# SBUF start addresses: where the moving operands of the matmuls begin within 128 bytes

## The reference, cut to what matters

```
first, for each of 2 layers:
  z = rms_norm(h) @ w_in                       # 1024 -> 2624
  y = [latent attention(z), retention(z)]      # w_q_b, w_kv_b inside
  h = h + y @ w_out
  h = h + (silu(hf @ gate) * (hf @ up)) @ w_down     # hf = rms_norm(h), 2816 wide
second, layer 0:  FFN, pooling mixer (pool_w), FFN   # each FFN 1024 -> 2*2816 -> 1024
second, layer 1:  FFN, differential attention (qkv, w_o), FFN
out = rms_norm(x, final_g)
```

## The kernel before

| tile | before | after |
|---|---|---|
| raw, w_hi, w_lo, R | 0 | 0 |
| xn_hi, xn_lo, sqb, tn, ssum | 0 | 64 |
| tab (constants) | 32 | 96 |
| mid_hi, mid_lo | 0 | 64 |
| dq, dk, oh, ol (second attention) | 64 | 64 |
| lat, zq, zk, zv (first attention), zp | 64 | 0 |
| krp, qf, v_ret | 0 | 64 |
| cn_hi, cn_lo (first row) | 0 | 0 |

## Time and profile before

### The profile page before, as it was taken

One profiled execution on the slowest core, in us unless ns is written; L12 is line 12 of the kernel. 1 busy time (PEld: TensorE's weight loads), 2 busy tenths in 40 slices (PEclk: granted clock), 3 DMA queues, 4 the chain that ended last, 5 costly groups with the idle time before them and its releaser, 6 DMA issues.

```text
span 2301.2 us, 37388 instructions
## 1 busy us (share of the span) xinstructions
PE 2258.3 (98%) x14172; PEld 2033.1 (88%) x14172; DVE 1462.8 (64%) x2310; ACT 847.0 (37%) x1130; POOL 160.2 (7%) x235
## 2 busy tenths in 40 slices
PE   8999999999999999999999999999999999999998
PEld 8999999999999988888888888888888888879998
DVE  4547777556778787678778767773333346556555
ACT  4445444435634432222432222232212234445443
POOL 0110000130000110001001101000000001000000
PEclk9999999999999999999999999999999999999999
DMA  6225665323665565455335545433233223123553
GB/s 230 98 74 195 206 239 174 124 83 103 210 237 187 180 207 183 164 192 177 106 130 204 182 162 199 160 115 110 77 105 109 71 95 127 56 74 128 173 192 128
DMA packets 65483, 343.21 MB, mean 149 GB/s; under 512 B 7152, under 2 KB 10480, under 8 KB 42608
## 3 DMA queue, kind: packets, MB, share of 16 engines
q1 hardware_dynamic: 44656, 266.47, 33.3%
q0 software_dynamic: 20736, 75.51, 9.8%
HBM read 340.90 MB, written 1.05 MB: 149 GB/s over the span
## 4 chain that ended last, share of the span: by engine, by line
PE 79%; issue 11%; DVE 6%; ACT 3%; DMA 1%; POOL 0%; DVEq 0%; SPq 0%; ACTq 0%; POOLq 0%
PE gpt L841 20%; PE gpt L843 19%; PE gpt L842 19%; DVE w_lo L1951 2%; ACT w_hi L1461 2%; PE gpt L938 1%; PE gpt L766 1%; PE gpt L939 1%; PE gpt L940 1%; PE gpt L767 1%; PE gpt L768 1%; PE mbt L1121 1%; PE gpt L1336 1%; PE gpt L1337 1%; PE gpt L1338 1%
## 5 line engine op out<-in xcount | busy, mean ns | idle before, releaser
L841 PE MATMUL gpt<-xn_hi,w_hi 128*128 128x512 f32 (+2 forms) x2256 | 747.3, 331 | 5.7 <-DVE w_lo L1951 5.7
L842 PE MATMUL gpt<-xn_lo,w_hi 128*128 128x512 f32 (+2 forms) x2256 | 742.8, 329 | 0.0
L843 PE MATMUL gpt<-xn_hi,w_lo 128*128 128x512 f32 (+2 forms) x2256 | 742.7, 329 | 0.0
L1951 DVE TENSOR_TENSOR w_lo<-raw,w_hi 128x2048 fp32r<-128x2048 f32 (+2 forms) x280 | 567.6, 2027 | 249.7 <-ACT w_hi L1461 249.5
L1461 ACT ACTIVATE w_hi<-raw 128x2048 fp32r<-128x2048 f32 (+2 forms) x280 | 476.4, 1702 | 390.9 <-PE gpt L843 356.5
L841 PEld LDWEIGHTS gpt<-xn_hi,w_hi 128*128 128x128 f32 x2256 | 426.5, 189 | 46.6 <-issue 7.1
L842 PEld LDWEIGHTS gpt<-xn_lo,w_hi 128*128 128x128 f32 x2256 | 426.6, 189 | 37.6
L843 PEld LDWEIGHTS gpt<-xn_hi,w_lo 128*128 128x128 f32 x2256 | 426.5, 189 | 37.5
L841 PE MATMUL gpt<-mid_hi,w_hi 128*128 128x512 f32 (+2 forms) x996 | 333.1, 334 | 4.7 <-DVE mid_lo L2149 4.5
L842 PE MATMUL gpt<-mid_lo,w_hi 128*128 128x512 f32 (+2 forms) x996 | 332.2, 334 | 0.0
L843 PE MATMUL gpt<-mid_hi,w_lo 128*128 128x512 f32 (+2 forms) x996 | 332.2, 334 | 0.0
(11 more groups left out here) (341 smaller groups left out, 2734.5 us busy)
## 6 DMA issues: line engine op xcount, KB each, us to landing
raw<-in_up_a SPq DMA_DIRECT2D x72, 1024.0 KB, 4.7
ada_w<-in_ada POOLq DMA_DIRECT2D x144, 512.0 KB, 3.5
raw<-in_up_b SPq DMA_DIRECT2D x60, 1024.0 KB, 4.8
raw<-in_down_a SPq DMA_DIRECT2D x48, 768.0 KB, 4.3
raw<-in_down_b SPq DMA_DIRECT2D x48, 640.0 KB, 3.9
raw<-in_win SPq DMA_DIRECT2D x16, 1024.0 KB, 4.8
raw<-in_qkv SPq DMA_DIRECT2D x12, 1024.0 KB, 4.8
raw<-in_wout SPq DMA_DIRECT2D x8, 1024.0 KB, 4.8
```

Source lines behind the costliest of these rows:

```text
L841: mm(o, w_hi[b][:, j, :], hi(k), start=(k == 0), stop=False)
L842: mm(o, w_hi[b][:, j, :], lo(k), start=False, stop=False)
L843: last = mm(o, w_lo[b][:, j, :], hi(k), start=False, stop=(k == kt - 1))
L1951: V.tensor_tensor(w_lo[b][:, 0:tiles, :], raw[b][:, 0:tiles, :], w_hi[b][:, 0:tiles, :].bitcast(F32), ALU.subtract).then_inc(lo_ready, 1)
```

## The change

Four unused tiles ("gaps") are laid between the others. The first, of 192 bytes, moves all that lies behind `R`; three more, of 832 bytes, stand ahead of the FFN's middle tiles, the second attention's tiles and its output tiles, and the middle tiles lose their alignment of 128. No instruction, loop, wait or transfer is added or taken away.

```diff
--- before.py
+++ after.py
@@ -157,6 +157,7 @@
         w_lo = [sb(f"w_lo{b}", [P, SIDE_T, P], F32R) for b in range(2)]
         ada_w = [sb(f"ada_w{b}", [P, D]) for b in range(2)]
         R = sb("R", [P, KT, TALL])
+        sb("gap_x", [P, 48])
         xn_hi = sb("xn_hi", [P, KT, T2], F32R)
         xn_lo = sb("xn_lo", [P, KT, T2], F32R)
         sqb = sb("sqb", [P, 4, T2])
@@ -181,8 +182,9 @@
 
 
         with ExitStack() as ffn_mem:
-            mid_hi = sb("mid_hi", [P, FF_A, T2], F32R, ffn_mem, 128)
-            mid_lo = sb("mid_lo", [P, FF_A, T2], F32R, ffn_mem, 128)
+            sb("gap_m", [P, 208], F32, ffn_mem)
+            mid_hi = sb("mid_hi", [P, FF_A, T2], F32R, ffn_mem)
+            mid_lo = sb("mid_lo", [P, FF_A, T2], F32R, ffn_mem)
             sg = sb("sg", [P, 2, T2], F32, ffn_mem)
             midf = sb("midf", [P, 2, T2], F32, ffn_mem)
         with ExitStack() as mix1:
@@ -216,6 +218,7 @@
         with ExitStack() as mix2:
             zp = sb("zp", [P, 4, 2, SEQ], F32, mix2)
         with ExitStack() as mix3:
+            sb("gap_d", [P, 208], F32, mix3)
             dq = sb("dq", [P, DHEADS, SEQ], F32, mix3)
             dk = sb("dk", [P, DHEADS, T2], F32, mix3)
             dvn = sb("dvn", [P, 4, D], F32, mix3)
@@ -224,6 +227,7 @@
             dy = sb("dy", [P, T2], F32, mix3)
             dsm = sb("dsm", [P, 6, 32], F32, mix3)
         with ExitStack() as mix4:
+            sb("gap_o", [P, 208], F32, mix4)
             oh = sb("oh", [P, DHEADS, SEQ], F32R, mix4)
             ol = sb("ol", [P, DHEADS, SEQ], F32R, mix4)
         drot_a, drot_b = tn[:, :, 0:SEQ], tn[:, :, SEQ:T2]
```

## The result

The changed kernel takes 2319.30 us (median of 4 runs, 2311.06 to 2325.89), the kernel before 2305.54 (4 runs, 2301.33 to 2308.83): a ratio of 1.0063, with an interval of 1.0035 to 1.0091. The same kernel timed again with six runs gave 2317.18 against 2303.03, 1.0057 (1.0039 to 1.0075). The forecast was 2259 us, faster; the sign was wrong.

What follows compares the result with a forecast made beforehand. TensorE, busy 98% of the span, was taken to bound the kernel through distances between matmuls. 30.0 + 18.0 - 0.1 = 47.9 us off the 2301.2 us span gave 2253.3, with 6.0 added 2259; range 2218 to 2297.

Steps and rivals of the forecast that it cites:

- Nothing: Rival: alignment isn't the cause and `oh` is fast for another reason; 2307 us, chance 0.09.
- (a): 512-column matmuls of `xn` and `mid`, moved from 0 to 64: 6.7 ns saved on each of 4476, 30.0 us.
- (b): 256-column matmuls, 0 to 64, and `v_part` with roles changed: 4.4 ns saved on each of 4080, 18.0 us.
- (c): 272-column matmuls: 0 taken, bounds from a loss of 2.3 us to a gain of 9.9.
- (d): Layer 1's `xn` at 16 tokens goes from 64 back to 0: 0.1 us lost.
- (e): First attention's tiles, pooling tile, constants and other small groups: nothing, 0.5 us either way.
- Slower: Rival: streams at 64 drift; 231.4 ns at 512 columns, 21.0 us lost less 9.0 won, 2319 us, chance 0.10.
- class of 117.8 ns: The weaker step read at remainder 64: last `oh` streak and layer 1's output projection, 117.8 ns against 120.0.
- The base: The median taken to lie 6.0 us above the profiled span: 2253.3 becomes 2259.

Runs made afterwards that it cites:

- experiments 1 and 4: 1: only streaks of 60 matmuls, moving tile's start varied, 226.7 and 228.9 ns at 512 columns; 4: `e_w192`.
- m3_circle: Only matmul streaks, no network: d (moving start less weight start) from 0 to 224, entry varied, plain float32 too; 226.7 to 234.4 ns at 512 columns.
- e_w192: Changed kernel with weights, raw slots and residual moved by 192 bytes too, so d = 0; 2302.87 us against 2304.84, ratio 0.9987.
- after: The changed kernel as first timed and profiled, against the kernel before; 2319.30 us, ratio 1.0063.
- after_again: The changed kernel run again unchanged, six runs, against the kernel before; 2317.18 us against 2303.03.

## Why the prediction was wrong

**What held.** The bound was read rightly: distances of TensorE decide, and they depend on an address. The rival "Nothing" is out (experiments 1 and 4). The runs also speak against what the prediction cited from the Trainium skill, "SBUF — State Buffer", Who interferes with whom, that TensorE's port for the moving operand and the one for the weights are independent, in so far as it means that their addresses don't matter: for float32r the distance changes with the difference of the two starts though no other engine runs (226.7 to 234.4 ns in `m3_circle`). How the two reads meet inside TensorE or SBUF no run shows.

**The step that failed: (a), 512 columns.** The prediction took "the better step of the 256-column rows, a saving of half of it, 6.7 ns", as the excess was the same 13.4 ns at both widths. The equal excess was read as one cost with one cure. That was a step without a row behind it. Measured, it is +6.7 ns: 29.1 us lost in place of 30.0 won, a swing of 59.1. Against the forecast span of 2253.3 us the miss is 56.0: these 59.1, 7.1 more in (b), 6.3 less in (c) and 3.6 less in (d) and (e), together 56.3. At d = -64 256 columns gain and 512 lose; the width takes part in the pattern. The bounds of (a), nothing and 13.4 ns, held no loss at all, though the rival "Slower" worked one out from the earlier trace rows; a row at another width, taken as a bound, had to leave both signs open.

**The reading beneath it.** The prediction had it that "at equal alignment each matmul loses 32 cycles", and at 64 apart less: the fitting key was d by 256 with its sign. The prediction put and the earlier trace rows into one class; by 256 the first two are at -64, while in the third `xn` is at +64 and `cn`, whose rows are 1088 bytes apart, at all four remainders in turn. Its class of 117.8 ns was at least two cases, d = +64 and the weaker step of d = -64. And "Nothing at remainder 0 runs in steps of 113.5 for long" tells of 256 columns alone; at 512 equal starts are the fastest.

**(b), 256 columns: mechanism right, less left at the end.** The up parts that no wait disturbed fell to 113.5 or 117.8 ns, the two steps that the prediction had from `oh` (forecast 115.6 between them), and over all 256-column distances under 150 ns the mean fell by 4.9 ns, 23.2 us. `v_part` and `mix_in`, with the roles changed, have d = +64, since weights move there and `xn` stands still; their mean went from 119.8 to 117.2. But 12.3 us came back: 6.5 in distances with idle time of TensorE, 5.3 of it waits for `w_lo` and `mid_lo`, 5.5 as half clock, and 0.3 in other long distances; 10.9 us net. The half clock isn't the price of the change, as its total of 27.3 us is that of before. Without it (b) would be 16.4, near its forecast of 18.0, and the gains of (c) and of the others would be smaller by some 3 us each, an estimate from half of the 6.0 and 5.8 us that they ran less at half clock. The prediction took the 504 matmuls out where cover was gone, rightly (65.8 to 65.6 us), but put the growing waits elsewhere at nothing: for `w_lo` ahead of the down part and behind it (0.4 us in the second half of up, 1.9 for 1.3 at the next stage), and for `mid_lo` where the two down parts of the second layer begin (1.3 and 2.7 us for 0.7 and 2.0).

**(c), 272 columns: 0 forecast, 6.3 us won.** 125.5 fell to 123.5 ns, inside the bounds, and `m3_circle` gives 123.4 ns for this width at d = -64. Distances under 150 ns became 1.7 ns shorter on the mean, 4.3 us over some 2570. The half clock took some 3.0 less (6.0 us of it instead of 12.0, reckoned as above), and longer distances gave about 1 back. **(d) and (e)** came to 3.5 us less over all other kinds, where 0.6 was allowed. Reckoned the same way, 2.9 of them are the clock: 9.5 us ran at half clock instead of 15.3. The moved constants and other tiles show no gain: `e_w192` keeps them where the change put them, and its "all others" take 304.1 us (302.8 before). The `oh` streaks stayed at their steps, as forecast. Timeline of after, 45 steps of the longest one, 113.3 ns each, beside the earlier trace rows:

```profile
2091.91 0.28 PE L1368 MATMUL gpt<-oh,w_lo 128*128 128x256 f32 x1
...
2097.01 0.28 PE L1368 MATMUL gpt<-oh,w_lo 128*128 128x256 f32 x1
```

**The slower rival** held in its price (2319) and in its test ("over 109.8": 112.0), but not in its mechanism. The price agrees by luck: it counts 21.0 us lost and 9.0 won, where 29.1 were lost and 20.7 won over all other kinds. The stream does not drift: it settles, in some stages into 233, 233, 234 ns over and over, in others into 231 and 236 in turn, and both are about 233.3 on the mean. It was given 0.10 because the regularity of `oh` was held against it; a step can be as regular and longer.

**The base.** 6.0 us were added to the span. In every timed execution, those of the kernel before too, 1.6 to 1.8 us lie outside it; the rest of the 6.0 was the distance of one execution from the median.

## What to carry to other kernels

Where float32r matmuls run back to back, the start of each moving row less the start of the weights, by 256 and with its sign, was worth 3 to 6% of their distance here; find it out for each width with streaks of sixty, entered in more than one way, before a layout is moved. Here 512 columns wanted equal starts and 256 and 272 wanted the moving row 64 bytes behind, and one tile served both by an offset inside its row (2295.12 us). A rate read at one width bounds nothing at another, and a gain in a stage that waits for its producers comes back in part as longer waits.

## What the runs showed that was not expected

- The same stream, at the same addresses, has two lasting steps, 113.3 and 117.8 ns (256 columns, d = -64), and how it is entered chooses between them. In the kernel the choice differs between executions, and between two halves of one FFN in the same execution. What exactly sets it is open.
- At d = 0 nothing of this kind is seen: 226.7 and 120.0 ns in every run. In the streaks, some other differences came back changed when the entry changed.
- Plain float32 shows no dependence on the start, and its distance a record is two passes over the columns: 429.2 ns at 512 and 215.8 at 256. The Trainium skill, "TensorE: Matmul & The Clock Gate", Back-to-back issue gap, has columns / 2.4 + 2.5 ns for an isolated warm matmul, an estimate of 429.2 and 215.8 for 1024 and 512 columns: the runs agree. No float32r distance reaches its 215.8 for 512 columns.
- Before the clock of 0.50 at 725.70 of after lay waits of 2.7 us, and 29 matmuls in 6.1 us. The kernel before waited 2.0 us at the same place without a fall of the clock, and `e_w192` waited 2.0 us with one. What decides it is open.
- Why the medians of after lie 6 to 8 us above its first profiled execution is open in part. That execution had the shorter step of 256 columns in more places than the profiled one of `after_again` (603.7 against 607.6 us). Of its three other runs two had a mean clock of 0.989, but in `after_again` the times did not follow the clock.
